# Both MLPs: weight-block sums a pair ahead, the last hidden difference and six products ahead of the first addition

## The reference, cut to what matters

```
def sq_relu_mlp(h, w1, w2):
    return jnp.square(jax.nn.relu(h @ w1)) @ w2
...
        h = modulate(rms_norm(x, W['norm2_w'][l]), sh2, sc2)
        x = x + gt2 * sq_relu_mlp(h, W['mlp_w1'][l], W['mlp_w2'][l])
```

## Time and profile before

| | |
|---|---|
| time, median of 3 runs | 2367.96 us (2361.13 to 2368.38) |
| the profiled execution's own time | 2364.42 us |
| its span | 2362.4 us |
| mean granted TensorE clock | 0.96 |
| PE busy | 2116.8 us (90%) |
| DVE busy | 1388.0 us (59%) |
| ACT busy | 1033.4 us (44%) |
| POOL busy | 310.2 us (13%) |
| DMA, share of 16 engines | 20.5% |

### The profile page before, as it was taken

The page is one execution under the profiler, slowest core; times in us unless marked ns, Lnnn a source line. Parts: engine busy times, 40 slices in busy tenths (PEclk is TensorE's granted clock), DMA queues, the critical chain, the costliest instruction groups (busy, mean ns, idle before and its releaser), DMA issues. The chain is left out here.

```text
span 2362.4 us, 59241 instructions
## 1 busy us (share of the span) xinstructions
PE 2116.8 (90%) x25699; PEld 1801.1 (76%) x25699; DVE 1388.0 (59%) x2656; ACT 1033.4 (44%) x1864; POOL 310.2 (13%) x542
## 2 busy tenths in 40 slices
PE   6999878888999999879995888888888989999998
PEld 3678654578999999834884776677776789999998
DVE  3142566536748484762515778777784368485746
ACT  4242454335434435371324555555653254434353
POOL 1000230010000000100001444444442100000000
PEclk9999999989999999969996999999998999999999
DMA  7221209911221222121110000000001211222212
GB/s 271 72 72 38 74 20 331 370 36 54 72 90 54 90 72 72 36 82 52 72 36 10 7 6 10 7 9 10 9 7 41 72 62 65 90 71 73 85 59 81
DMA packets 127982, 167.78 MB, mean 71 GB/s; under 512 B 13788, under 2 KB 85228, under 8 KB 127596
## 3 DMA queue, kind: packets, MB, share of 16 engines
q1 hardware_dynamic: 127724, 164.00, 20.5%
HBM read 160.44 MB, written 3.54 MB: 69 GB/s over the span
## 5 line engine op out<-in xcount | busy, mean ns | idle before, releaser
L171 PE MATMUL psum<-arena 64*64 64x64 f32 (+6 forms) x17072 | 831.4, 247 | 137.1 <-DVE arena L2180 15.9
L171 PEld LDWEIGHTS psum<-arena 64*64 64x64 f32 (+3 forms) x17072 | 662.6, 145 | 348.5 <-issue 153.7
L171 PE MATMUL psum<-hidden_high,weights_high 128*128 128x320 f32 x896 | 281.6, 314 | 30.6 <-DVE weights_low L758 19.2
L171 PE MATMUL psum<-hidden_high,weights_low 128*128 128x320 f32 x896 | 278.9, 311 | 0.0
L171 PE MATMUL psum<-hidden_low,weights_high 128*128 128x320 f32 x896 | 278.7, 311 | 0.0
L171 PE MATMUL psum<-norm_low,weights_high 128*128 128x320 f32 x992 | 226.7, 310 | 0.0
L171 PE MATMUL psum<-norm_high,weights_high 128*128 128x320 f32 x992 | 226.6, 310 | 0.0
L171 PE MATMUL psum<-norm_high,weights_low 128*128 128x320 f32 x992 | 226.4, 310 | 0.0
L171 PEld LDWEIGHTS psum<-hidden_high,weights_high 128*128 128x128 f32 x896 | 170.0, 190 | 37.0 <-DVE weights_low L758 25.6
L171 PEld LDWEIGHTS psum<-hidden_low,weights_high 128*128 128x128 f32 x896 | 170.1, 190 | 0.0
L171 PEld LDWEIGHTS psum<-hidden_high,weights_low 128*128 128x128 f32 x896 | 169.9, 190 | 0.0
(11 more groups left out here) (228 smaller groups left out, 3385.6 us busy)
## 6 DMA issues: line engine op xcount, KB each, us to landing
weights<-in_mlp_w SPq DMA_DIRECT2D x64, 1024.0 KB, 5.3
arena<-in_ada_w SPq DMA_DIRECT2D x24, 2048.0 KB, 9.1
arena<-in_ab_w_in SPq DMA_DIRECT2D x6, 2048.0 KB, 7.7
arena<-in_ab_w_out SPq DMA_DIRECT2D x2, 2048.0 KB, 8.6
arena<-in_rwkv_wv SPq DMA_DIRECT2D x2, 2048.0 KB, 8.1
arena<-in_rwkv_wr SPq DMA_DIRECT2D x2, 2048.0 KB, 8.3
arena<-in_rwkv_wk SPq DMA_DIRECT2D x2, 2048.0 KB, 8.0
arena<-in_rwkv_wo SPq DMA_DIRECT2D x2, 2048.0 KB, 8.6
```

Of the source, the lines that this page charges most:

```text
L171: return nc.tensor.matmul(out, lhsT, rhs, start=start, stop=stop, skip_group_check=shared)
```

## The change

Four things are altered, for all eight groups:

- WALK: the last steps of products 3 and 5 of pair 0 (six matmuls) move ahead of product 6. DONE, and so the evacuations and the low parts, becomes 1, 2, 3, 5, 6, 7, (1,1), 4 in pair 0; it was 1, 2, 6, 5, 3, 7, (1,1), 4.
- The evacuation of (0,1) moves out of hidden(grp, 3), behind its part 1.
- The sums of pair 0 are formed in the turn of up block 2 and those of pair 1 in the turn of up block 3, behind the six low parts of pair 0; those of pairs 2 and 3 are formed, all three parts at once, behind the evacuation of (0,4) and of (1,4).
- Each part of weight_sums waits for the low parts that read its own blocks, where part 0 waited for all.

```diff
-        WALK = [(0, q, 0, 3) for q in (1, 5, 2, 3)] + [(0, q, 3, 4) for q in (1, 2)]
-        WALK += [(0, 6, 0, 4), (0, 5, 3, 4), (0, 3, 3, 4), (0, 7, 0, 4), (1, 1, 0, 4), (0, 4, 0, 4)]
+        WALK = [(0, q, 0, 3) for q in (1, 5, 2, 3)] + [(0, q, 3, 4) for q in (1, 2, 3, 5)]
+        WALK += [(0, 6, 0, 4), (0, 7, 0, 4), (1, 1, 0, 4), (0, 4, 0, 4)]
...
-        SUMS_DONE = [max(n for n, (i, j) in enumerate(PREPARED) if i == d and j in S_OF) + 1 for d in range(4)]
+        SUMS_USED = ((W_S3, W_S1), (W_S2,), (W_S4,))
+        SUMS_DONE = [[max(PREPARED.index((d, j)) for j in js) + 1 for js in SUMS_USED] for d in range(4)]
...
+            if n:
+                dve.wait_ge(S("slot_low"), 28 * group_n(l, grp - (i == 0)) + SUMS_DONE[i - 1][part])
             if part == 0:
                 wait_loaded(dve, g)
-                if n:
-                    dve.wait_ge(S("slot_low"), 28 * group_n(l, grp - (i == 0)) + SUMS_DONE[i - 1])
...
                 for part in range(2):
-                    if b == 3 and part:
-                        evacuate(grp, 0, 1)
                     dve.wait_ge(S("hidden_high"), 4 * n + 3 + part)
...
                     else:
-                        for part in range(3):
-                            weight_sums(dve, l, grp, 0, part)
                         for j in range(6):
                             slot_low(dve, l, grp, 0, j)
+                    if b >= 2:
+                        for part in range(3):
+                            weight_sums(dve, l, grp, b - 2, part)
                     hidden(grp, b)
                 for i, q in DONE:
-                    if (i, q) != (0, 1):
-                        evacuate(grp, i, q)
-                    else:
+                    evacuate(grp, i, q)
+                    if (i, q) == (0, 1):
                         slot_low(dve, l, grp, 0, W_A22)
+                    if i < 2 and q == 4:
+                        for part in range(3):
+                            weight_sums(dve, l, grp, i + 2, part)
                     if i < 3:
-                        if q == 1:
-                            weight_sums(dve, l, grp, i + 1, 0)
-                        elif q in (5, 2) and DONE.index((i, q)) == 7 * i + 1:
-                            weight_sums(dve, l, grp, i + 1, 1)
-                            weight_sums(dve, l, grp, i + 1, 2)
                         slot_low(dve, l, grp, i + 1, Q_OF[q][0])
```

## The result

The changed kernel takes 2388.8 us (median of 4 runs, 2386.1 to 2393.7), the kernel before 2367.7 us: a ratio of 1.0092, 95% interval 1.0075 to 1.0108. It is slower by 21 us, where 14.5 us over the profiled execution had been forecast. The time lies outside the forecast's 2373 to 2384 us, at the upper edge, 2389, of all that was held possible. The sign and the mechanisms of pair 0 came out; the size was too small.

What follows compares the result with a forecast made beforehand. It took the DVE work ahead of the evacuation of (0,6) as the bound, and summed 2364.4 + 4.2 (sums) + 9.5 (clock) + 0.8 (POOL) = 2378.9 us. Forecast case 2373 to 2384, range 2366 to 2389.

Steps and rivals of the forecast that it cites:

- What bounds it: Pair 0 of each down stage: the DVE work ahead of the evacuation of (0,6) sets the end.
- part 2: Before product 7: 2.45 us taken out, 2.96 put in; restart as before, one hole of 3.88 us.
- Part 1: Before product 6 of pair 0: the first hole, 1.19 us, goes, hidden by six moved matmuls.
- part 3: Before product 4 of pair 0: the third hole, 0.62 us, goes.
- Part 4: Before (1,7) and (2,7): sums in one piece make new holes; a stage ends 0.53 us later, eight 4.2.
- The clock: Behind product 7's restart: all eight stages fall to half clock, 1.53 us each, +9.5 us in all.
- the bound from above: Clock behind product 7's restart: part of the low stretch may last twice as long, +15.7 us.
- Layer 0's last group: One low part lengthened by POOL's adding of squares falls ahead of the evacuation of (1,6): +0.8 us once.
- (a): Rival, product 7's restart: clock stays up in the stages where it did, 2371.3 us; chance 0.16.
- (c): Rival, pair 0: product 7 restarts 2.45 us earlier, 2346 us; chance 0.10 with its milder form.
- (b): Rival, product 7's restart: low clock lasts twice as long in half of the stages, 2385.1 us; chance 0.10.
- (d): Rival, up block 3: sums of pair 1 don't fit and hold back hidden(3), 8 us per microsecond beyond; chance 0.02.

Runs made afterwards that it cites:

- 2.96 us less: The changed kernel with product 6 of pair 0 again ahead of the last steps of products 5 and 3: 2355.7 us.
- the sums left in: The kernel before with only the new order of products; sums and the evacuation of (0,1) stay where they were: 2403.6 us, one run.
- the kernel with one wait: The changed kernel with one wait at the head of the sums in place of one for each part: 2383.3 us, one run.
- the version with product 5 last: The 2344 us kernel (old product order, sums of pairs 2 and 3 split) with product 5's last step behind product 7, squares asked for late: 2345.1 us.
- the sums spread: The changed kernel with the sums of pairs 2 and 3 in two pieces again, as before the change: 2381.7 us.

## Why the prediction was right or wrong

**What bounds it** was right: the string of 5.68 us, and product 7's restart at 12.68 us into the stage against 12.62. The two sides of it were then tried alone: 2.96 us less gave 9.74, the sums left in gave 15.57. One remark in part 2 is wrong: 0.57 us are said to come back from part 1. The L866 half of 0.73 leaves the string and the string starts 0.30 later, which is 0.43; the sum of 5.68 doesn't use it.

**Part 1 and part 3**, the first and third hole gone: right, no row with idle time at either place.

**Part 4, the sums of pairs 2 and 3**: right in kind, too small. The holes are 0.71 and 0.72 late, not 0.56 and 0.53. The term that was too small is the block of sums: 2.72 us against the 2.59 taken from the earlier trace rows, because the added waits of parts 1 and 2 were listed as costing nothing. With one wait the holes are 0.58. With the short fall, a stage comes to 110.29 + 0.53 + 1.53 = 112.35 by the prediction, 112.38 in the kernel with one wait, and 112.67 in the changed one. That makes 0.3 us a stage, 2.2 us in seven.

**The clock**: all eight stages fall, as said, and a fall costs 1.55 us (1.53). The long stretches were the bound from above, given a chance of their own and left out of the sum: two of eight came, 0.9 us more each, 1.8 us. That all stages fall was a likely outcome and not a certain one, as the stage without a fall in the kernel with one wait shows.

**Layer 0's last group** is where the largest part of the miss lies. The prediction gave it 0.8 us more for POOL, from one lengthened low part. From its stage of 56.12 us that would make 56.12 + 0.53 + 0.62 + 0.8 = 58.1; it took 62.0. The rows of DVE in that group after:

```profile
975.56 1.57 DVE L759 TENSOR_TENSOR weights_low<-weight_sums,weights_high 128x512 fp32r<-128x512 f32 x1
...
988.37 2.08 DVE L759 TENSOR_TENSOR weights_low<-weights,weights_high 128x512 fp32r<-128x512 f32 x1
...
990.96 1.44 DVE L759 TENSOR_TENSOR weights_low<-weight_sums,weights_high 128x512 fp32r<-128x512 f32 x1
992.32 0.66 DVE L873 SCALAR_TENSOR_TENSOR arena<-psum,ada,arena 128x192 f32<-128x192 f32 x2
```

and at pair 2 before the change, where L874 at 980.31 is the evacuation of (2,6), as L873 at 992.32 is after it:

```profile
978.33 2.06 DVE L758 TENSOR_TENSOR weights_low<-weight_sums,weights_high 128x512 fp32r<-128x512 f32 x1
980.31 0.66 DVE L874 SCALAR_TENSOR_TENSOR arena<-psum,ada,arena 128x192 f32<-128x192 f32 x2
980.90 1.45 DVE L758 TENSOR_TENSOR weights_low<-weight_sums,weights_high 128x512 fp32r<-128x512 f32 x1
```

The first is the one foreseen. At pair 2, POOL's two additions had met one low part in the string before and now meet two, since the sums push the low parts into them. The prediction read pair 1 alone and did not look at these rows of pair 2. This makes the hole of 2.86, and the hole in its turn brings the clock down for 6.8 us: from (2,7) to (3,7) PE takes 15.14 us in place of 12.40, so 2.7 of the 5.9 us that the group loses are this fall. The miss is 3.9 us.

2.2 + 1.8 + 3.9 = 7.9, and 14.5 + 7.9 = 22.4, against 22.5 in the MLP stages of the trace. The time itself was missed by 2388.8 - 2378.9 = 9.9 us, of which 3.3 are the base: the sum starts at the profiled execution's 2364.4, and the median before is 2367.7. The failing steps are terms of the sum: a wait priced at nothing, a contention looked at for one instruction and not for the string behind it, and the second length of the low stretch.

**The rivals.** (a), the clock stays up, and (c), an earlier restart, are ruled out by the rows. (b), low for twice as long, came in two of eight stages. (d), the sums of pair 1 holding back block 3, did not come: DVE has 1.98 us to spare there.

```profile
2209.18 0.82 DVE L852 TENSOR_TENSOR hidden<-hidden 128x640 f32<-128x640 f32 x1 [1.98 <-ACT hidden L803]
```

## What to carry to other kernels

Where PE waits for one result of a busy in-order engine, add up all that stands ahead of that result on the engine, from the last moment at which the engine was idle, with start-to-start distances from the trace. In these runs PE's restart followed the order there, to 0.1 us in three kernels, and a piece that is moved has to be followed to the next wait too, as the version with product 5 last shows. Several short holes with work between them were cheaper here than one long one, because the long one also brought the clock down, for 1.5 to 2.7 us each time.

## What the runs showed of the hardware that I had not expected

- A satisfied wait in front of a DVE instruction is not free when DVE is the bound: 0.13 us for two of them in a block of 2.6 us.
- The same idle time of 3.7 us ahead of product 7 had different sequels: a low stretch of 3.4 us in six stages of the changed kernel and of 6.8 in two, of 6.8 in all eight with the sums spread, and none in one stage of the kernel with one wait. What picks the length in a given stage was not tried, and stays open.
- DVE's low parts that ran beside POOL's additions of 128x640 took between 1.44 and 2.08 us in the changed kernel, in place of 0.69. When the additions were asked for later, other low parts were lengthened, those that then ran beside them.
